# A bidirectional mLSTM layer with a mixture of experts: the recurrence's state-free work formed ahead of it, and the recurrence in units of four heads

## The reference

```python
b = jnp.cumsum(fc, axis=-1)
logw = jnp.where(mask, b[..., :, None] - b[..., None, :] + ic[..., None, :], -jnp.inf)
inter_log = b + m[..., None]
m_row = jnp.maximum(inter_log, jnp.max(logw, axis=-1))
s = jnp.einsum('bhjd,bhsd->bhjs', qc, kc) * jnp.exp(logw - m_row[..., None])
inter = jnp.exp(inter_log - m_row)
num = jnp.einsum('bhjs,bhsd->bhjd', s, vc) + inter[..., None] * jnp.einsum('bhed,bhjd->bhje', C, qc)
den = jnp.sum(s, axis=-1) + inter * jnp.einsum('bhd,bhjd->bhj', n, qc)
h = num / jnp.maximum(jnp.abs(den), jnp.exp(-m_row))[..., None]
C_new = decay[..., None, None] * C + jnp.einsum('bhs,bhse,bhsd->bhed', u, vc, kc)
n_new = decay[..., None] * n + jnp.einsum('bhs,bhsd->bhd', u, kc)
```

## Time and profile before

| | us |
|---|---|
| median of the runs (lowest, highest) | 1279.34 (1278.87, 1282.72) |
| the profiled execution | 1283.91 |
| its span, first to last instruction | 1282.2 |
| TensorE, VectorE, ScalarE, GpSimd busy in the span | 1159.6, 876.6, 687.0, 185.2 |

### The profile page before, as it was taken

The page is one execution under the profiler, slowest core; times in us unless marked ns, Lnnn a source line. Parts: engine busy times, 40 slices in busy tenths (PEclk is TensorE's granted clock), DMA queues, the critical chain, the costliest instruction groups (busy, mean ns, idle before and its releaser), DMA issues.

```text
span 1282.2 us, 18679 instructions
## 1 busy us (share of the span) xinstructions
PE 1159.6 (90%) x6071; PEld 980.2 (76%) x6071; DVE 876.6 (68%) x1410; ACT 687.0 (54%) x1122; POOL 185.2 (14%) x260
## 2 busy tenths in 40 slices
PE   5999999999999979999299999999999999999920
PEld 4887888888799968887178788888888888888810
DVE  4639510110188845665579999999999999999958
ACT  4431231221165653233277877787778777877733
POOL 1100200000010211212202211221122212211100
PEclk9999989999999989999599999999999999999965
DMA  8212230210011054552779999999999999999757
GB/s 228 56 33 74 97 109 1 66 33 33 1 50 51 2 165 134 162 181 98 261 239 359 369 382 384 378 373 389 388 383 381 390 382 385 375 383 383 276 225 303
DMA packets 119699, 287.30 MB, mean 224 GB/s; under 512 B 22448, under 2 KB 53680, under 8 KB 119648
## 3 DMA queue, kind: packets, MB, share of 16 engines
q1 hardware_dynamic: 103744, 245.02, 52.5%
q0 software_dynamic: 15904, 41.61, 8.9%
HBM read 261.76 MB, written 37.92 MB: 234 GB/s over the span
## 4 chain that ended last, share of the span: by engine, by line
PE 50%; DVE 7%; ACT 3%; DMA 2%; issue 2%; POOL 0%; ACTq 0%; SPq 0%; POOLq 0%; DVEq 0%
PE psum L643 15%; PE psum L645 14%; PE psum L644 14%; DVE e_lo L1543 3%; ACT e_hi L1113 3%; PE psum L857 2%; PE psum L815 1%; PE psum L890 1%; DVE x L1660 1%; DVE x L1668 1%; DVE x L1658 1%; PE psum L803 1%; DMA gx<-xn_scratch,rows_to 1%; DMA f_y<-expert_rows 0%; PE psum L782 0%
## 5 line engine op out<-in xcount | busy, mean ns | idle before, releaser
L1543 DVE TENSOR_TENSOR e_lo<-e_st,e_hi 128x1024 fp32r<-128x1024 f32 x384 | 442.5, 1217 | 16.9 <-ACT e_hi L1113 15.8
L1113 ACT ACTIVATE e_hi<-e_st 128x1024 fp32r<-128x1024 f32 x384 | 372.3, 1050 | 10.4 <-PE psum L645 9.5
L643 PE MATMUL psum<-e_hi,ex_hi 128*128 128x512 f32 x512 | 204.5, 399 | 8.9 <-DVE ex_lo L1591 3.7
L644 PE MATMUL psum<-e_lo,ex_hi 128*128 128x512 f32 x512 | 200.9, 392 | 0.0
L645 PE MATMUL psum<-e_hi,ex_lo 128*128 128x512 f32 x512 | 200.7, 392 | 0.0
L643 PE MATMUL psum<-xT_hi,w_hi 128*128 128x512 f32 (+1 forms) x408 | 147.5, 362 | 6.9 <-DVE w_lo L1227 3.8
L644 PE MATMUL psum<-xT_lo,w_hi 128*128 128x512 f32 (+1 forms) x408 | 146.3, 359 | 0.0
L645 PE MATMUL psum<-xT_hi,w_lo 128*128 128x512 f32 (+1 forms) x408 | 146.0, 358 | 0.0
L643 PEld LDWEIGHTS psum<-e_hi,ex_hi 128*128 128x128 f32 x512 | 96.7, 189 | 41.8 <-DVE e_lo L1543 16.5
L645 PEld LDWEIGHTS psum<-e_hi,ex_lo 128*128 128x128 f32 x512 | 96.8, 189 | 21.0
L644 PEld LDWEIGHTS psum<-e_lo,ex_hi 128*128 128x128 f32 x512 | 96.9, 189 | 19.1
(11 more groups left out here) (233 smaller groups left out, 1876.5 us busy)
## 6 DMA issues: line engine op xcount, KB each, us to landing
e_st<-in_expert_w_gate_dram SPq DMA_DIRECT2D x128, 512.0 KB, 5.8
e_st<-in_expert_w_up_dram SPq DMA_DIRECT2D x128, 512.0 KB, 6.4
e_st<-in_expert_w_down_dram SPq DMA_DIRECT2D x128, 512.0 KB, 8.5
w_st<-in_w_in_dram SPq DMA_DIRECT2D x20, 512.0 KB, 4.2
xn_scratch<-xn POOLq DMA_DIRECT2D x20, 512.0 KB, 3.8
f_y<-expert_rows SPq DMA_DIRECT2D x20, 512.0 KB, 12.3
out_dram<-x SPq DMA_DIRECT2D x10, 512.0 KB, 4.8
x_in<-in_x_sample_dram POOLq DMA_DIRECT2D x8, 512.0 KB, 5.5
```

What stands on the lines that cost most here:

```text
L643: pe.matmul(out, a_hi, b_hi, start=start, stop=False)
L644: pe.matmul(out, a_hi, b_lo, start=False, stop=False)
L1113: act.activation(e_hi[:, r, :, :], e_st[:, slot, :, :], ACT.Copy).then_inc(ehi_done, 1)
L1543: dve.tensor_tensor(e_lo[:, r, :, :], e_st[:, slot, :, :], e_hi[:, r, :, :].bitcast(F32), ALU.subtract).then_inc(elo_done, 1)
```

## The change

All work that needs no state is formed once for each chunk and pair of heads, a block, for both directions together, beside the Q projections of the second and third segment (eight blocks) and the V tiles (twelve). TensorE only transposes the keys and forms the scores. The two gate rows go through DRAM (rows_dram) and are loaded by DMA, broadcast over the partitions; GpSimd puts the mask on them, ScalarE forms the exponentials, VectorE the products. Weighted scores, weighted queries and backward keys are stored in DRAM (units_dram, back_keys_dram); the forward keys stay in kT. A block's buffers are one of three stages, later five. The last two slices of w_in are issued between the blocks' transfers.

The recurrence has 20 units, one step and one direction with all four heads. SyncE loads each unit's operands (512 KB, with the backward keys 768 KB) into four buffers, the first two units' into a region of their own, and w_out's slices between them. h is formed by ScalarE (scaled copies), the sum of the directions by VectorE. Units that start a scan don't multiply by the state, and units that end one don't form it. The first tile's head norm, mixf and its parts are formed between the last units, and its loads are issued at unit 14. The output stage's buffers move, and the identity and mask constants in bf16 go. The diff, cut:

```diff
+    rows_dram = nc.dram_tensor("gate_rows", (8 * (H // 2), T), F32).ap()
+    units_dram = nc.dram_tensor("mlstm_units", (NT, P, 2, 2, H * P), F32).ap()
+    back_keys_dram = nc.dram_tensor("back_keys", (NT, P, H * P), F32).ap()
...
+    b_wgt = [at(f"b_wgt{i}", o[0], [P, 2, 2, P], F32) for i, o in enumerate(stages)]
+    b_qi = [at(f"b_qi{i}", o[1], [P, 2, 2, P], F32) for i, o in enumerate(stages)]
+    b_key = [at(f"b_key{i}", o[2], [P, 2, P], F32) for i, o in enumerate(stages)]
...
+    units = [at(f"units{i}", Q0 + 6 * KB * i if i < 3 else V0, [P, 3 * H, P], F32) for i in range(4)]
...
-        NU = 4 * NT
+        NU = 2 * NT
         def unit(n):
-            step, pair, d = n // 4, n // 2 % 2, n % 2
-            return step, pair, d, chunk_of(step, d)
+            step, d = n // 2, n % 2
+            return step, d, chunk_of(step, d)
...
+        BLOCKS = [(c, pair) for c in dict.fromkeys(chunk_order) for pair in range(H // 2)]
+        NB = len(BLOCKS)
+        NQ = NPROJ - H * (NS - 1)
+        N_EARLY = H * (NS - 1)
+        def blocks_after(n):
+            return (n - NQ,) if NQ <= n < NPROJ else ()
+        def blocks_with(t):
+            spread = [N_EARLY, N_EARLY + 2] + [N_EARLY + 2 + i for i in range(1, NT - 1)] + [NB]
+            return range(spread[t], spread[t + 1])
+        def stage_of(i):
+            return i % 3 if i < N_EARLY else (i - N_EARLY) % 5
...
+            def block_in(i):
+                ck, pair = BLOCKS[i]
+                st = stage_of(i)
+                if i == 0:
+                    sp.wait_ge(rows_out, 16 * 4 * H // 2)
+                    for j in range(4):
+                        sp.wait_ge(ev_out[j], 16 * len(ring[j::4]))
+                if st >= 3:
                     sp.wait_ge(wlo_done, NSL)
-                else:
+                wait(sp, blk_out[st], 48 * stage_uses(i))
+                if st == 4:
+                    sp.wait_ge(blk_out[0], 48 * sum(stage_of(j) == 0 for j in range(N_EARLY)))
+                for kind, dst in ((0, b_wgt[st]), (1, b_qi[st])):
+                    a = 8 * pair + 4 * kind
+                    sp.dma_start(dst[:, :, :, :].rearrange("p d h n -> p (d h) n"),
+                                 rows_dram[a:a + 4, ck * P:(ck + 1) * P].unsqueeze(0)
+                                 .broadcast_to([P, 4, P])).then_inc(blk_in[st], 16)
+            def block_out(i):
+                ck, pair = BLOCKS[i]
+                st = stage_of(i)
+                heads = slice(2 * pair * P, (2 * pair + 2) * P)
+                sp.wait_ge(s_done, i + 1)
+                for kind, src in ((0, b_wgt[st]), (1, b_qi[st])):
+                    sp.dma_start(units_dram[ck, :, :, kind, heads],
+                                 src[:, :, :, :].rearrange("p d h n -> p d (h n)")).then_inc(blk_out[st], 16)
+                sp.dma_start(back_keys_dram[ck, :, heads],
+                             b_key[st][:, :, :].rearrange("p h n -> p (h n)")).then_inc(blk_out[st], 16)
...
+            def unit_load(n):
+                step, d, ck = unit(n)
+                if n >= 6:
+                    sp.wait_ge(num_ready, n - 3)
+                    wait(sp, kv_ready, states_kept(n - 3))
+                src = units_dram[ck, :, d, :, :].rearrange("p k (h n) -> p (k h) n", n=P)
+                keys = back_keys_dram[ck].rearrange("p (h n) -> p h n", n=P)
+                arrived = tile_in[unit_sem(n)]
+                if n < 2:
+                    at_tile = [slice((2 * n + x) * P, (2 * n + x + 1) * P) for x in range(2)]
+                    sp.dma_start(first_units[:, 0:6, at_tile[0]], src[:, 0:6, :]).then_inc(arrived, 16)
+                    sp.dma_start(first_units[:, 0:2, at_tile[1]], src[:, 6:8, :]).then_inc(arrived, 16)
+                    if d:
+                        sp.dma_start(first_units[:, 2:6, at_tile[1]], keys).then_inc(arrived, 16)
+                    return
+                slot = units[(n - 2) % 4]
+                sp.dma_start(slot[:, 0:2 * H, :], src).then_inc(arrived, 16)
+                if d:
+                    sp.dma_start(slot[:, 2 * H:3 * H, :], keys).then_inc(arrived, 16)
...
+            for i in range(3):
+                block_in(i)
+            for i in range(NB):
+                if i in (N_EARLY // 2, N_EARLY // 2 + 1):
+                    slice_in(NSL - 2 + i - N_EARLY // 2)
+                block_out(i)
+                if i + 2 < N_EARLY and i >= 1:
+                    block_in(i + 2)
+                if i == N_EARLY - 1:
+                    for j in range(N_EARLY, N_EARLY + 4):
+                        block_in(j)
+                elif i >= N_EARLY and i + 4 < NB:
+                    block_in(i + 4)
+                if i == NB - 4:
+                    sp.wait_ge(proj_ready, NPROJ + 4)
+                    for n in range(2):
+                        unit_load(n)
+            for st in range(5):
+                sp.wait_ge(blk_out[st], 48 * sum(stage_of(j) == st for j in range(NB)))
+            for n in range(2, 6):
+                unit_load(n)
+                if n < 4:
+                    wo_in(n - 2)
+            for n in range(6, NU):
+                unit_load(n)
+                if n % 2 and n // 2 - 1 < KD:
+                    wo_in(n // 2 - 1)
+                if n == 14:
+                    sp.wait_ge(hss_done, 2)
+                    for i in range(2):
+                        mixer_in(i)
+            sp.wait_ge(h_done, NU)
+            sp.wait_ge(state_done, states_kept(NU))
+            x_again(0)
+            sp.dma_start(g2_b[:, :], norm2_g[0:1, :].broadcast_to([P, D])).then_inc(g2_in, 16)
+            x_again(1)
+            for i in range(2, NT):
+                mixer_in(i)
+                x_again(i)
...
-            for t in order:
-                pool.wait_ge(h_done, complete_after(t))
-                pool.tensor_tensor(h_fb[:, 0, t, :], h_fb[:, 0, t, :], h_fb[:, 1, t, :], ALU.add).then_inc(hsum_done, 1)
+            for i in range(NB):
+                pool.wait_ge(blk_in[stage_of(i)], 32 * (stage_uses(i) + 1))
+                for d, sign in enumerate((1, -1)):
+                    logw = b_wgt[stage_of(i)][:, d, :, :]
+                    ins = pool.affine_select(out=logw, in_=logw, compare_op=ALU.is_ge, fill=MASKED, base=0,
+                                             pattern=[[0, 2], [sign, P]], channel_multiplier=-sign)
+                ins.then_inc(masked, 1)
...
+            def block_scores(i):
+                ck, pair = BLOCKS[i]
+                tok = slice(ck * P, (ck + 1) * P)
+                if i == 0:
+                    pe.wait_ge(cols_done, 1)
+                    pe.wait_ge(act_took, act_results(NQ))
+                if i == N_EARLY:
+                    pe.wait_ge(act_took, act_results(NPROJ))
+                if i >= 4:
+                    pe.wait_ge(s_done, i - 3)
+                for hh_ in range(2):
+                    pe.transpose(psum[:, 4 + i % 4, hh_ * P:(hh_ + 1) * P], kT[:, 2 * pair + hh_, tok], ident[:, :])
+                for hh_ in range(2):
+                    last = pe.matmul(psum[:, 4 + i % 4, (2 + hh_) * P:(3 + hh_) * P], kT[:, 2 * pair + hh_, tok],
+                                     qT[:, 2 * pair + hh_, tok], start=True, stop=True)
+                last.then_inc(kq_ready, 1)
...
             def unit_rows(n):
+                step, d, ck = unit(n)
+                pe.wait_ge(tile_in[unit_sem(n)], units_signalled(unit_sem(n), n + 1))
                 if n >= 2:
                     pe.wait_ge(h_done, n - 1)
+                    wait(pe, state_done, states_kept(n - 1))
+                for h in range(H):
+                    out = psum[:, 4 * (n % 2) + h // 2, (h % 2) * (P + 1):(h % 2 + 1) * (P + 1)]
+                    if not from_zero(step):
+                        pe.matmul(out, unit_part(n, H + h), state[:, d, h, :], start=True, stop=False)
+                    last = pe.matmul(out, unit_part(n, h), v[:, ck, h, :], start=from_zero(step), stop=True)
+                last.then_inc(num_ready, 1)
+                for h in range(H):
+                    keys = unit_part(n, 2 * H + h) if d else kT[:, h, ck * P:(ck + 1) * P]
+                    if carries(step):
+                        last = pe.matmul(psum[:, 4 * (n % 2) + 2 + h // 2, (h % 2) * (P + 1):(h % 2 + 1) * (P + 1)],
+                                         keys, v[:, ck, h, :], start=True, stop=True)
                 if carries(step):
+                    last.then_inc(kv_ready, 1)
...
+            pe.wait_ge(v_took, NT)
+            pe.wait_ge(v_ones, 1)
+            pe.wait_ge(s_done, NB)
+            for n in range(NU):
+                unit_rows(n)
+                if n == NU - 2:
+                    pe.wait_ge(state_done, states_kept(n))
+                    h_transposes(0)
...
+            def block_weights(i):
+                ck, pair = BLOCKS[i]
+                act.wait_ge(masked, i + 1)
+                for d in range(2):
+                    for hh_ in range(2):
```

(111 more changed lines are left out.)

327 lines of the change are left out of this document (125 added, 202 removed).

## The result

The changed kernel took 1245.57 us (median of 4 runs, 1245.11 to 1247.61), the kernel before 1280.65 us (4 runs, 1278.87 to 1282.72): ratio 0.9724, 95% interval 0.9709 to 0.974. The forecast was 1245. The profiled execution after took 1245.86 us, with a span of 1244.1.

The account below looks back on a forecast made before the run. TensorE's instruction count was taken to bound the recurrence. Recurrence and hand-over fall from 112.3 to 65.6 us; with +13.3 for blocks and -0.7 that is -34.1 us, giving 1245 us in the median, range 1231 to 1263.

Parts of the forecast that it names:

- the rival with TensorE as bound: Recurrence: the wo chain and norms hide in slack and TensorE stays the bound; -48 us, 1231 us, chance 0.10.
- units 0 and 1 with the wait for unit 2: Start of the recurrence: 32 instructions from zero state, 3.6 us, then a 1.8 us wait for unit 2's load.
- step 1: Recurrence, second step: unit 4 lands 6.1 us after unit 2, and the step takes that.
- steps 2 to 7 with the norms: Middle of the recurrence: six steps at 6.1 us, 36.6 us, plus 5.0 us for the first head norms.
- step 8: Recurrence step without a w_out slice: 5.3 us.
- the end: From unit 18 to the first output matmul: matmuls, denominators, sums, mixf, mix_hi, mix_lo and signals, 7.2 us.
- the wo chain: Recurrence: VectorE's wo_lo waits for ScalarE's wo_hi and delays the next unit; 6.1 us a step, TensorE 0.8 us short.
- the norms: ScalarE's first head norms before the copies of units 7 and 10 in the recurrence: together 5.0 us more.
- The transfers: Rival: DMA at 230 GB/s sets the recurrence's pace, 8.0 us a step, and slows early blocks; -16 us, 1263, chance 0.20.
- dropping GpSimd's constants and VectorE's row splitting saves nothing: Work left out by the change: no gain, since TensorE is busy meanwhile.
- TensorE waits 3.3 us at this place already: End of Q: the last V weight part comes about 3.5 us after TensorE finishes; existing wait 3.3 us, so no change.
- two blocks in flight: First eight blocks beside Q: 8.4 us from a stage's release to its product, two in flight, so 4.2 us a block.

Follow-up runs that it names:

- the doubled products: Changed kernel with each product of keys and values for the state issued twice (128 more TensorE instructions in the recurrence): 1249.94 us, 0.975 to the kernel before.
- wo_lo later: Changed kernel with VectorE's low part of each w_out slice formed one unit later, behind the next unit's denominators and state: 1242.81 us, 0.9701 to the kernel before.
- 3 of 17 MB gone: Changed kernel without the loads of w_out's slices 2 to 7, so its output differs: 1242.07 us, 0.9689 to the kernel before.
- Loads ahead of stores: Changed kernel with early block i+2's broadcast rows asked for ahead of block i's three stores on the same queue: 1241.88 us, 0.9683 to the kernel before.
- weight first: Kernel before, with VectorE forming the low part of weight slice 8 ahead of the stabilised gate rows: 1283.80 us, 1.0018 to the kernel before.

## Why the prediction was right

**TensorE's work** was counted rightly: 416 instructions in the recurrence, and 303 for 240 in the V stage, which took 63.4 us where the forecast's terms give 63.8 (57.8 + 60 x 0.111 - 0.7). An instruction of the recurrence took 0.119 us, not 0.111 (50.06 us for 420), so that a full step of 48 needs 5.7 us on TensorE and not 5.3.

**The recurrence** came as forecast, 64.4 us for 65.6, and the rival with TensorE as bound is refuted by the doubled products. It came so term by term. TensorE's first product of units 0, 2, 4, 16 and 18:

```profile
355.76 1.16 PE L918 MATMUL psum<-v,first_units 128*128 128x129 f32 x8 [0.75 <-ACT v L1199]
...
361.24 0.49 PE L917 MATMUL psum<-state,units 128*128 128x129 f32 x2 [1.64 <-DMA units<-mlstm_units]
...
366.97 1.16 PE L918 MATMUL psum<-v,units 128*128 128x129 f32 x8 [0.43 <-DMA units<-mlstm_units]
...
407.08 0.46 PE L917 MATMUL psum<-state,units 128*128 128x129 f32 x2 [1.05 <-ACT h_fb L1245]
...
412.51 0.39 PE L917 MATMUL psum<-state,units 128*128 128x129 f32 x2
```

With the first output matmul at 420.26 that is 5.5 us for units 0 and 1 with the wait for unit 2 (forecast 5.4), 5.7 for step 1 (6.1), 40.1 for steps 2 to 7 with the norms (41.6), 5.4 for step 8 (5.3) and 7.8 for the end (7.2). VectorE's eight wo_lo start at 363.7 to 409.5 us, 6.5 us apart in the mean with the norms in it. What the forecast has no number for is what a term is worth when it is taken away. It put the wo chain at 0.8 us a step over TensorE's own work, 4.8 us in six steps, and the norms at 5.0; taken away one at a time each gave about 3. Something else then ends last: with wo_lo later ScalarE's waits for w_out grow by 4.2 us, and TensorE's own 5.7 us a step lie close to the chain's 6.1. Which of these takes how much was not measured. The transfers come close too (0.76 of the engines' time, w_out landing in 6.4 us), but with 3 of 17 MB gone the kernel gained 4.7 us and not 8 to 12.

**"... dropping GpSimd's constants and VectorE's row splitting saves nothing, since TensorE is the busy one meanwhile"** failed. TensorE is the busy one over the stage, but between 97 and 145 us of the kernel before VectorE has hardly a gap (46.2 of 48 us busy), and TensorE stood 2.4 us for a weight part behind that split. It is worth 2.2 to 2.4 us of TensorE's time in the slices of 118 to 126 us, 4.1 us by the medians.

**"TensorE waits 3.3 us at this place already, for that same part: no change"** failed too. The wait became 4.8 us, for ScalarE's last take of Q, which stands in its queue behind block 6's weights. GpSimd's masks, each released by a block's rows, show the pace of the blocks (4, 5 and 6 here; the next came 4.8 us later): up to 7.5 us a block and not 4.2.

```profile
274.24 0.76 POOL L728 TENSOR_SCALAR_AFFINE_SELECT b_wgt<-b_wgt 128x256 f32<-128x256 f32 x2 [5.24 <-DMA b_qi<-gate_rows]
281.70 0.76 POOL L728 TENSOR_SCALAR_AFFINE_SELECT b_wgt<-b_wgt 128x256 f32<-128x256 f32 x2 [6.70 <-DMA b_qi<-gate_rows]
287.86 0.76 POOL L728 TENSOR_SCALAR_AFFINE_SELECT b_wgt<-b_wgt 128x256 f32<-128x256 f32 x2 [5.39 <-DMA b_qi<-gate_rows]
```

Block 6's own chain, from the issue of its loads at 281.63 to the end of its product at 290.72, took 9.1 us, near the forecast's 8.4. The forecast divided it by two blocks in flight, but left out that on SyncE's queue a block's loads stand behind an earlier block's stores, which wait for that block's product. Loads ahead of stores got 4 to 6 us back. There the next limit shows, which the forecast left out as well: a stage is free only when its last block's stores have landed (SyncE's waits for them ahead of the loads are 10.3 us between 250 and 300 us, and 1.0 in the changed kernel).

**Errors that cancelled.** In the profiled executions V started at 292.4, not 296. By ScalarE's second take of K TensorE was 5.9 us ahead of the kernel before (180.87 for 186.77): 2.4 us by the row split, and some 3.4 by a fall of the clock (0.72 over 168 to 180 us) that the kernel before's profiled execution holds and the changed kernel's doesn't. The fall is not the change's: executions of the changed kernel and its edits had 1.00, 0.86 or 0.72 there. From there to V's start the change cost 9.1 us, where the forecast had 6.7: 1.4 us of longer wait, and most of the rest for the two blocks behind it, which ran at the fallen clock. Without the fall the spans differ by 34.7 us. That this is so near the forecast's 34.1 is partly luck: 2.4 us won and 2.4 us lost, neither of them counted on, cancelled.

## What to carry to other kernels

Ask of each stretch, not of each stage, which engine has no gap: work dropped from that one can count even where TensorE is nearly full. On one queue, put the loads that someone will wait for ahead of stores that nobody waits for yet. A piece of in-order work that waits for another engine belongs behind the next unit's urgent work, on the same engine; on a slower one it keeps its buffer longer, and here the wait came back as a late load. And where several chains lie within a microsecond of each other, do not expect the full price of one back when it is taken away.

## What the runs showed of the hardware

The granted clock fell to 0.50 in 172 to 176 us of the kernel before while TensorE was busy all 4.00 us of that slice and of those on either side:

```profile
168.00:172.00 4.00, 4.00 (x47) 3.87 (x46) 1.75 (x2) 1.44 (x2) 0.54 (x1) 0.92 0.83 229
...
176.00:180.00 4.00, 4.00 (x15) 3.18 (x14) 0.00 (x0) 0.00 (x0) 0.00 (x0) 0.73 0.01 4
```

So a fall came without a wait. Just before it TensorE worked through very narrow instructions: 30 transposes of 36 columns (L707), from 168.64 us on, and 16 products of 10 columns (L711). In each of the 11 profiles, of 14, that hold this fall it begins during this run of narrow instructions or within 1 us of its end, also in "weight first", where the run comes at 172.23 us and the fall in the slice of 174. Three profiles hold the run and no fall, so it comes in some executions and not in others of one program: the changed kernel showed 1.00, 1.00 and 0.86 over 168 to 180 us. That the narrow instructions are its cause was not tested. A difference of 3 us between two profiles can be just this fall.
